# Residual projections with wide weight panels in a two-block transformer kernel on one core

## What is computed

```python
# first block, layer l
mix = jnp.concatenate([o_att, o_hg.astype(x.dtype), o_cv], axis=-1)   # 512 + 256 + 256 features
x = x + mix @ w_out[l]
h = rms_norm(x, norm_mlp[l])
x = x + jnp.square(jax.nn.relu(h @ w_mlp_in[l])) @ w_mlp_out[l]       # 4096 hidden
# second block, layer l
y = jnp.concatenate([mix, mo], axis=-1) @ w_out[l]
x = _layer_norm(DN_ALPHA * x + y, ln_mix_g[l], ln_mix_b[l])
```

## Time and profile before

| what | value |
|---|---|
| median of 3 runs | 3034.63 us (3034.35 to 3037.44) |
| the profiled execution | 3036.94 us |
| its span, first to last instruction | 3035.1 us |
| TensorE busy, mean granted clock | 2805.1 us (92%), 0.955 |
| VectorE busy | 1823.4 us (60%) |
| ScalarE busy | 1291.3 us (43%) |
| memory read / written | 467.51 / 37.75 MB |

### The profile page before, as it was taken

The page is one execution under the profiler, slowest core; times in us unless marked ns, Lnnn a source line. Parts: engine busy times, 40 slices in busy tenths (PEclk is TensorE's granted clock), DMA queues, the critical chain, the costliest instruction groups (busy, mean ns, idle before and its releaser), DMA issues.

```text
span 3035.1 us, 47180 instructions
## 1 busy us (share of the span) xinstructions
PE 2805.1 (92%) x19276; PEld 2552.8 (84%) x19276; DVE 1823.4 (60%) x3074; ACT 1291.3 (43%) x1473; POOL 154.3 (5%) x74
## 2 busy tenths in 40 slices
PE   7888999878999889999999999897898999999998
PEld 7756999648998589899999988786898899999886
DVE  4764645764535369974555556646599845554565
ACT  4434534434434435444444444443354444444443
POOL 1000001000000041000000000000320000000000
PEclk9988999979999799999999999998999999999999
DMA  6301554103454143465566567541434656656672
GB/s 244 114 1 56 183 179 152 69 1 117 175 181 159 44 155 140 194 255 185 211 209 219 196 234 267 188 158 61 149 140 181 238 195 220 214 200 213 227 266 97
DMA packets 72897, 507.30 MB, mean 167 GB/s; under 512 B 8096, under 2 KB 8368, under 8 KB 18096
## 3 DMA queue, kind: packets, MB, share of 16 engines
q1 hardware_dynamic: 58576, 424.70, 39.0%
q10 hardware_dynamic: 5472, 47.03, 3.8%
q0 software_dynamic: 8704, 33.56, 3.2%
HBM read 467.51 MB, written 37.75 MB: 166 GB/s over the span
## 4 chain that ended last, share of the span: by engine, by line
PE 86%; DVE 10%; issue 2%; ACT 2%; DMA 1%; ACTq 0%; DVEq 0%
PE lin L1346 16%; PE lin L1347 16%; PE lin L1348 16%; PE m L1346 8%; PE m L1347 8%; PE m L1348 8%; PE m L1688 4%; PE m L1440 2%; DVE lo L768 1%; PE m L1433 1%; PE m L1418 1%; DVE st L934 1%; PE m L1395 1%; PE m L1506 1%; PE m L1341 1%
## 5 line engine op out<-in xcount | busy, mean ns | idle before, releaser
L768 DVE TENSOR_TENSOR lo<-raw,hi 128x2048 fp32r<-128x2048 f32 x381 | 872.1, 2294 | 746.9 <-ACT hi L391 738.8
L1346 PE MATMUL lin<-xh,hi 128*128 128x256 f32 x3408 | 981.3, 288 | 21.2 <-DVE lo L768 11.2
L391 ACT ACTIVATE hi<-raw 128x2048 fp32r<-128x2048 f32 x403 | 769.3, 1910 | 525.9 <-PE m L1348 343.1
L1347 PE MATMUL lin<-xl,hi 128*128 128x256 f32 x3408 | 970.7, 285 | 0.0
L1348 PE MATMUL lin<-xh,lo 128*128 128x256 f32 x3408 | 970.4, 285 | 0.0
L1346 PEld LDWEIGHTS lin<-xh,hi 128*128 128x128 f32 x3408 | 660.8, 194 | 29.7 <-DVE lo L768 17.7
L1347 PEld LDWEIGHTS lin<-xl,hi 128*128 128x128 f32 x3408 | 660.9, 194 | 4.4 <-issue 1.2
L1348 PEld LDWEIGHTS lin<-xh,lo 128*128 128x128 f32 x3408 | 660.1, 194 | 0.0
L1346 PE MATMUL m<-hi,ah 128*128 128x512 f32 x1024 | 399.8, 390 | 0.0
L1347 PE MATMUL m<-lo,ah 128*128 128x512 f32 x1024 | 399.2, 390 | 0.0
L1348 PE MATMUL m<-hi,al 128*128 128x512 f32 x1024 | 398.4, 389 | 0.0
(11 more groups left out here) (304 smaller groups left out, 3108.9 us busy)
## 6 DMA issues: line engine op xcount, KB each, us to landing
raw<-stream SPq DMA_DIRECT2D x403, 1024.0 KB, 4.8
gate_table<-stg ACTq DMA_DIRECT2D x16, 2048.0 KB, 6.3
g<-gate_table POOLq DMA_DIRECT2D x32, 1024.0 KB, 8.3
rows<-rows ACTq DMA_DIRECT2D x4, 1024.0 KB, 7.2
x_scratch<-x ACTq DMA_DIRECT2D x2, 1024.0 KB, 4.2
x<-x_scratch ACTq DMA_DIRECT2D x2, 1024.0 KB, 7.0
x<-mem SPq DMA_DIRECT2D x1, 1024.0 KB, 7.5
x<-x ACTq DMA_DIRECT2D x1, 1024.0 KB, 8.0
```

The lines of the kernel that those rows point to most:

```text
L391: act.activation(HI[i % SLOTS][:], RAW[:, i % SLOTS, :], ACT.Copy).then_inc(hi_ready, 1)
L768: dve.tensor_tensor(LO[i % SLOTS][:], RAW[:, i % SLOTS, :], HI[i % SLOTS][:].bitcast(F32), ALU.subtract).then_inc(lo_ready, 1)
L1346: pe.matmul(out_, ah, bh, start=first, stop=False, **kw)
L1347: pe.matmul(out_, ah, bl, start=False, stop=False, **kw)
```

## The change

The residual projections of both blocks get panels of another shape: 512 features by 512 columns, still 1 MB. `wide` replaces `half` for them. For each row tile it issues 4 feature tiles x 3 products with 512 moving columns into a bank of its own, 24 matmuls a panel, and a panel fills two banks: bank i0 + 2n + tt for column half n and row tile tt. A projection goes through the column halves 0 and 1 for each group of 512 features.

In the first block's out-projection the group of features 512 to 1023 comes first and waits for the first half of `XL` alone. In down each panel waits for the four hidden tiles that it needs. The residual adds take one bank each, a row tile of 512 columns; the two of column half n wait until the third (n = 0) or fourth (n = 1) of the last four panels has been used. In the second block each is followed by one `bn_stats` of 512 columns.

```diff
             def residual(h):
                 for u in range(4):
-                    i = h + u
+                    n, tt = divmod(u, 2)
                     if u >= 2:
                         lo_to(h + 4 + u - 1)
-                    dve.wait_ge(hp_used, i + 1)
-                    xv = X[:, :, 256 * u:256 * u + 256]
-                    dve.tensor_tensor(xv, xv, PS[i % 4][:].rearrange("p (t n) -> p t n", t=2), ALU.add).then_inc(bank_free[i % 4], 1)
+                    dve.wait_ge(hp_used, h + 3 + n)
+                    xv = X[:, tt, 512 * n:512 * n + 512]
+                    dve.tensor_tensor(xv, xv, PS[(h + u) % 4][:], ALU.add).then_inc(bank_free[(h + u) % 4], 1)
...
-                    dve.wait_ge(hp_used, i + 1)
-                    xv = X[:, :, 256 * u:256 * u + 256]
-                    dve.scalar_tensor_tensor(out=xv, in0=xv, scalar=DN_ALPHA, in1=PS[i % 4][:].rearrange("p (t n) -> p t n", t=2),
-                                             op0=ALU.mult, op1=ALU.add).then_inc(bank_free[i % 4], 1)
+                    dve.wait_ge(hp_used, s0 + N_MIX2[l] + 3 + n)
+                    xv = X[:, tt, 512 * n:512 * n + 512]
+                    dve.scalar_tensor_tensor(out=xv, in0=xv, scalar=DN_ALPHA, in1=PS[i % 4][:], op0=ALU.mult, op1=ALU.add).then_inc(bank_free[i % 4], 1)
                     evicted(dve, i)
-                    for tt in range(TT):
-                        ins = dve.bn_stats(STATS[:, tt, u, :], X[:, tt, 256 * u:256 * u + 256])
+                    ins = dve.bn_stats(STATS[:, tt, n, :], xv)
                 v.step(ins)
-                layer_norm(2 * l + 1, 4)
+                layer_norm(2 * l + 1, 2)
...
+            def wide(i, i0, n, hh, hl, k0, first, last):
+
+                pe.wait_ge(lo_ready, i + 1)
+                wh, wl = (t[i % SLOTS][:].rearrange("p (k n) -> p k n", k=KT // 2) for t in (HI, LO))
+                for tt in range(TT):
+                    j = i0 + 2 * n + tt
+                    if first and reads_before(j) > 0:
+                        pe.wait_ge(bank_free[j % 4], reads_before(j))
+                    for k in range(KT // 2):
+                        ins = three(PS[j % 4][:], hh[:, k0 + k, P * tt:P * tt + P], hl[:, k0 + k, P * tt:P * tt + P], wh[:, k, :], wl[:, k, :],
+                                    first and k == 0, last and k == KT // 2 - 1, skip_group_check=True)
+                ins.then_inc(hp_used, 1)
...
-                pe.wait_ge(sem("mixl_ready"), 2 * l + 2)
+                pe.wait_ge(sem("mixl_ready"), 2 * l + 1)
                 for u in range(N_OUT):
-                    half(h0 + N_IN + u, "rr")
+                    if u == 2:
+                        pe.wait_ge(sem("mixl_ready"), 2 * l + 2)
+                    wide(h0 + N_IN + u, h0 + N_IN, u % 2, XH, XL, 4 - 4 * (u // 2), u < 2, u >= 2)
...
-                pe.wait_ge(sem("hid_ready"), 16 * (l + 1) + 2)
                 for u in range(N_DOWN):
-                    half(h2 + u, "rr", 0, HH, HL, 8 * (u // 4), u < 4, u >= N_DOWN - 4)
+                    pe.wait_ge(sem("hid_ready"), 16 * l + 2 * (u // 2) + 4)
+                    wide(h2 + u, h2, u % 2, HH, HL, 4 * (u // 2), u < 2, u >= N_DOWN - 2)
...
                 for u in range(N_OUT):
-                    half(s0 + N_MIX2[l] + u, "rr")
+                    wide(s0 + N_MIX2[l] + u, s0 + N_MIX2[l], u % 2, XH, XL, 4 * (u // 2), u < 2, u >= 2)
...
+def _wide_panels(w, order):
+
+    k = w.shape[0] // 512
+    return np.concatenate([w.reshape(k, 4, P, 2, 512)[a].transpose(2, 1, 0, 3) for a in order], 0).reshape(2 * k, P, HP)
```

More of the change, by code:

```diff
@@ L1819, in layout_first @@
         parts.append(_half_panels(f("w_in")[l][:, oi]))
-        parts.append(_half_panels(f("w_out")[l][oo]))
+        parts.append(_wide_panels(f("w_out")[l][oo], (1, 0)))
         parts.append(_half_panels(f("w_mlp_in")[l]))
-        for kc in range(4):
-            parts.append(_half_panels(f("w_mlp_out")[l][1024 * kc:1024 * kc + 1024]))
+        parts.append(_wide_panels(f("w_mlp_out")[l], range(8)))
     par = np.concatenate([
@@ L1851, in layout_second @@
         parts.append(_half_panels(w_in))
-        parts.append(_half_panels(f("w_out_2")[l]))
+        parts.append(_wide_panels(f("w_out_2")[l], (0, 1)))
         parts.append(_half_panels(f("peer_w_q_2")[l]))
```

## The result

| | median of 5 | lowest to highest | profiled execution | its span | mean clock |
|---|---|---|---|---|---|
| before | 3035.02 us | 3034.35 to 3037.44 | 3036.94 us | 3035.1 us | 0.955 |
| changed | 3021.31 us | 3018.26 to 3023.67 | 3021.48 us | 3019.7 us | 0.954 |

The changed kernel is faster by half a per cent: the medians differ by 13.7 us, and the ratio of the times is 0.9949, with a 95% interval of 0.9938 to 0.996 (12 to 19 us). The forecast was 3022.3 us.

The account below looks back on a forecast made before the run. TensorE, busy 92% of the span, was taken as the bound. Gains of 15.4, 5.8 and 4.9 us less costs of 5.6, 7.0 and 1.2 gave 12.3 us, from the median 3034.63 to 3022.3 us; range 3015 to 3030.

Parts of the forecast that it names:

- Width: 48 residual projection panels go from 256-column to 512-column matmuls, 5.76 to 5.44 us each: 15.4 us gained.
- Start of the out-projection: First block: the first two panels need only features 512 to 1023, so TensorE's wait for the last xl goes: 5.8 us gained.
- start of down: Each down panel needs only four hidden tiles, so TensorE's wait for the last hl in two layers goes: 4.9 us gained.
- End of the first block's out-projection: After the last matmul come add, lo, add instead of one add: 2.8 us a layer, 5.6 us lost in two.
- End of the second block's: Out-projection end: add, bn_stats, lo, add, bn_stats take 4.97 us instead of 1.51: 7.0 us lost for two.
- End of down: All lo's are asked for ahead of the adds, so only one add comes on top: 0.59 us each, 1.2 us lost.
- Rival A: In the projections a 512-column matmul costs two of 256, so width saves nothing: 3037.7 us, chance 0.06.
- rival B: Longer stops at the projections' ends also cost clock, with more half-rate work behind them: 9 us lost, 3031.3 us, chance 0.09.
- sign of more than 35 us: Over 35 us of half-rate work after the six residual projection ends would show that longer stops cost clock.
- Rival C: Without holes at the out-projection and down starts, lower-clock stretches behind them close: at most 5.1 us back, 3017.2 us, chance 0.09.

Follow-up runs that it names:

- two pieces: The changed kernel with each product of 512 moving columns issued as two of 256: 3035.24 us, ratio to the kernel before 0.9997.
- the longer stops: The changed kernel with two more lo subtractions between the last two adds of the four out-projections: 3038.45 us, ratio to the kernel before 1.0002.

## Why the prediction was right

1. **Width, 15.4 us.** Right: 5.44 us a panel, the expert stage's price, shown in down by the row and by two pieces, which gave 13.9 to 14.6 us back. The fixed part of 13.3 ns goes with the matmul and not with the stage. The Trainium skill, "TensorE: Matmul & The Clock Gate", section "Back-to-back issue gap", gives 2.5 ns, for an isolated matmul. By it the width would have given an estimated 2.9 us. The runs do not agree: two pieces gave 13.9 us back.

2. **Start of the out-projection, 5.8 us, and 3. start of down, 4.9 us.** Right: both waits are gone, and each came back alone, in size and, within 1 us, in time.

4. **End of the first block's out-projection, -5.6 us.** Right: add, lo, add; the stop went from 5.25 to 8.04 us, forecast 8.1. The row that the prediction gave for the 5.25 us belongs to the end of down; the right one has the same length.

5. **End of the second block's, -7.0 us.** Right: 4.96 us for a forecast 4.97; the stops went from 7.02 to 10.37 us, forecast 10.5, and cost 6.7 for two.

6. **End of down, -1.2 us.** Right: 5.25 to 5.84 us in layer 0, 1.0 to 1.6 us in layer 1.

By the measured sizes the sum is 15.4 + 5.8 + 4.9 - 6.7 - 5.6 - 1.2 = 12.6 us. The medians say 13.7, the two profiled executions 15.5. The rest, 2.9 us between the profiled executions, is a sum of small differences of both signs. The part ahead of the first out-projection, whose code is as before, ended 1.3 us earlier (252.12 to 250.78, last attention products). From the end of layer 1's stop behind the out-projection to the end of its stop behind down (717.68 to 911.12 before, 707.51 to 892.91 after) 8.0 us were gained, where the terms make 7.0. In the second block, the stretch behind the first layer's out-projection ran 1.9 us shorter, the one behind the second layer's 1.4 us longer. The changed kernel's runs spread by 5 us, and none of this was isolated. That the forecast came within 1 us of the measured median is therefore partly luck; that each term came within 0.3 us of its row is not.

**Rival A** fell by two pieces, **rival B** by the longer stops, although its sign of more than 35 us appeared (39.3). **Rival C**, the clock given back at the starts, came at one start at most, and the mean clock is 0.954 after and 0.955 before. Layer 1's down start is at the upper level now (1.00 over its first 6 us, 0.72 before), which may be the 1.0 us that layer 1 gained beyond the terms. But it was so too in the kernel that had its 2.45 us hole back (1.00), so the level there doesn't hang on the hole. The out-projection's start has its slow stretch as before (0.83 over 10 us before, 0.84 after).

The 13.8 us that the prediction listed as costs of the ends weren't all the price of wide panels, though the working treated them so. Of them 8.8 are the lo's that the program's order leaves between the adds, and went with them. And each first-block stop still held 1.8 us that signalling by row tile freed. The forecast of the change was right; that a third of its gross gain of 26.1 us was given back through the order of a few calls was shown only by the runs.

## What to carry to other kernels

When a change makes several results complete at once (here two banks with each of the last two panels), list what stands between their readers in the queue of the engine that reads them: an operation that used to be hidden under a panel can come to lie behind the last one. Move such work ahead of all readers, and count whether it fits under what still runs: 5.6 us of work does not hide under 5.44 us. Price a matmul from a row of its own shape: the line through two widths held when a stage went from one of them to the other, and missed by a factor of 1.7 (0.0667 for 0.1117 us) when it was drawn on to a third.

## What the hardware showed that was not expected

- Time per matmul in a full stream at the upper level, with a new 128 x 128 float32 stationary tile each: 0.1117 us at 128 columns, 0.1200 at 256, 0.2267 at 512. From 256 to 512 it is the columns at 2.4 GHz and 13.3 ns; at 128 something else is the bound, and whether it is the weight load is not shown.
- The stream of 128-column matmuls didn't lift the clock. Three out-projections began at 1.2 GHz and stayed there from start to end, 81.8 us each with TensorE busy without a hole (clock 0.50); in the projection behind the first of them, whose matmuls have 256 columns, it was at the upper level again. Down and the fourth out-projection, which began at the upper level, kept it with the same 128-column stream (1.00). Why the level was held in both directions is open; no further run was made on it.
- A longer stop cost its own length alone: stops of 8.0 and 10.4 us, made 12.7 and 15.0 us long, left the half-rate time after them about as it was, 22.5 us for 24.1 at four places. That time after one and the same end varies by up to 6 us from kernel to kernel (5.3 to 11.5 us behind down in layer 1), and what sets it is open.
